# Gated delta rule inside a two-layer encoder trunk: pairs of the triangular inverse by a predicated copy, spreading copies replaced by zero-step weights, and the tail of the last head behind the first transposition

## What is computed

```python
for l in range(DEPTH):                     # DEPTH = 2
    x = x + 0.5 * swiglu(rmsnorm(x, ffn1_norm[l]), ...)        # D_FF = 2816
    x = x + hybrid_mixer(rmsnorm(x, mix_norm[l]), ...)
    x = x + 0.5 * swiglu(rmsnorm(x, ffn2_norm[l]), ...)
return rmsnorm(x, final_norm)

def hybrid_mixer(h, ...):
    proj = h @ w_in                        # q, k, v, g_out, a, b, glu, gates
    q, k, v = silu(short causal convolution of 4 taps of q, k, v), q and k l2-normed
    o = gated_delta_chunked(q, k, v, g, beta)      # 8 heads of 128
    y_a = (rmsnorm(o, head_norm) * silu(g_out)) @ w_a_out
    c = causal_depthwise_conv(val * sigmoid(gt), dw_conv_w) + dw_conv_b    # 31 taps
    y_b = silu(rmsnorm(c, conv_norm)) @ w_b_out
    return (sigmoid(gate_a) * y_a + sigmoid(gate_b) * y_b) @ w_o

def gated_delta_chunked(q, k, v, g, beta):
    gc = cumsum(g); decay = exp(gc_i - gc_j)
    m = (k * beta) @ k.T * decay_strict
    sol = triangular_solve(eye + m, [v * beta, k * beta * exp(gc)])
    attn = q @ k.T * decay_incl
    # then a scan over the chunks: v_new, o, state
```

## Time and profile before

| | us |
|---|---|
| runs of the kernel before | 3057.24, 3074.15, 3071.31 |
| median | 3071.31 |
| the profiled execution, its own time | 3066.26 |
| span of its instructions | 3064.5 |
| PE busy | 2902.3 (95%) |
| DVE busy | 1671.2 (55%) |
| ACT busy | 1107.7 (36%) |
| POOL busy | 345.8 (11%) |

### The profile page before, as it was taken

One profiled execution on the slowest core, in us unless ns is written; L12 is line 12 of the kernel. 1 busy time (PEld: TensorE's weight loads), 2 busy tenths in 40 slices (PEclk: granted clock), 3 DMA queues, 4 the chain that ended last, 5 costly groups with the idle time before them and its releaser, 6 DMA issues.

```text
span 3064.5 us, 41142 instructions
## 1 busy us (share of the span) xinstructions
PE 2902.3 (95%) x14080; PEld 2404.8 (78%) x14080; DVE 1671.2 (55%) x2475; ACT 1107.7 (36%) x1631; POOL 345.8 (11%) x308
## 2 busy tenths in 40 slices
PE   7999969999999999999999998699999999999999
PEld 6888847878887888888778886478887878788887
DVE  5554236878787345553255531388878863555532
ACT  3232235445454233322142322345554542332321
POOL 1000021211122010000000000221122220100000
PEclk9999979999999999999999999899999999999999
...
GB/s 143 96 96 96 66 106 120 104 99 103 100 108 80 101 94 91 98 97 93 78 103 96 94 95 62 115 102 99 114 105 86 117 74 106 91 94 97 94 91 69
DMA packets 479208, 296.79 MB, mean 97 GB/s; under 512 B 12180, under 2 KB 462868, under 8 KB 479092
## 3 DMA queue, kind: packets, MB, share of 16 engines
...
## 4 chain that ended last, share of the span: by engine, by line
PE 78%; issue 8%; DVE 5%; DMA 5%; ACT 3%; POOL 1%; DVEq 0%; ACTq 0%; POOLq 0%; SPq 0%
PE bank L414 76%; DMA raw<-in_w_in 4%; PE bank L542 2%; DMA w_lo<-raw 1%; ACT w_hi L751 1%; ACT w_lo L753 1%; DVE cacc L1185 1%; DVE dcol L1113 1%; DVE NT L1291 0%; DVE X L1244 0%; DVE XT L1302 0%; DVE XT L1244 0%; POOL attn L1559 0%; ACT hf L843 0%; DVE w_lo L1001 0%
## 5 line engine op out<-in xcount | busy, mean ns | idle before, releaser
L414 PE MATMUL bank<-h_hi,w_hi 128*128 128x512 f32 x2432 | 970.9, 399 | 27.8 <-DVE h_lo L1033 14.0
L414 PE MATMUL bank<-h_lo,w_hi 128*128 128x512 f32 x2432 | 984.2, 405 | 0.0
L414 PE MATMUL bank<-h_hi,w_lo 128*128 128x512 f32 x2432 | 966.0, 397 | 0.0
L751 ACT ACTIVATE w_hi<-raw 128x1024 fp32r<-128x1024 f32 x448 | 471.8, 1057 | 709.0 <-PE bank L414 621.9
L1001 DVE TENSOR_TENSOR w_lo<-raw,w_hi 128x1024 fp32r<-128x1024 f32 x336 | 412.1, 1228 | 553.9 <-ACT w_hi L751 553.0
L414 PEld LDWEIGHTS bank<-h_hi,w_hi 128*128 128x128 f32 x2432 | 463.7, 191 | 124.1 <-DVE h_lo L1033 15.5
L414 PEld LDWEIGHTS bank<-h_hi,w_lo 128*128 128x128 f32 x2432 | 463.9, 191 | 84.3
L414 PEld LDWEIGHTS bank<-h_lo,w_hi 128*128 128x128 f32 x2432 | 464.1, 191 | 82.6
L1185 DVE SCALAR_TENSOR_TENSOR cacc<-c_raw,ncol,cacc 128x512 f32<-128x512 f32 x464 | 352.4, 760 | 8.2
L414 PE MATMUL bank<-act_hi,w_hi 128*128 128x512 f32 x704 | 279.1, 396 | 0.0
L414 PE MATMUL bank<-act_lo,w_hi 128*128 128x512 f32 x704 | 279.1, 396 | 0.0
...
## 6 DMA issues: line engine op xcount, KB each, us to landing
raw<-in_w_in SPq DMA_DIRECT2D x128, 512.0 KB, 8.4
...
```

The lines of the kernel that those rows point to most:

```text
L414: return nc.tensor.matmul(o, a, b, start=start, stop=stop, **kw)
L751: nc.scalar.activation(w_hi[c % SLOTS][:, :], raw[c % SLOTS][:, :], ACT.Copy).then_inc(hi_done, 1)
```

## The change

- The gate's spread copy gbc (DVE) and the spread copies fbc (DVE, 16 in the heads and 8 in the norms) are gone. The matmuls take one column with a step of zero as their 128 columns of weights (`whole`).
- The mask decs (POOL) is gone; NT is made from the unmasked dec with a negated factor (a new small operation, neg). XT begins as the identity, which ACT writes (XTI), and one predicated copy puts the pairs in: it takes the place of m1 and x2T.
- tanh of v goes to a tile of its own, thv. Y is no longer negated.
- PE_ORDER has other places. x2t comes after 8 halves in place of 14, vt, y0 and fb behind it; four halves in place of three ahead of each xt, three in place of two ahead of os1, os2 and os3, two in place of three ahead of gr.
- On DVE the chain to x2T comes ahead of v, c_raw and dcol; the last head's oF, o_hi and o_lo move behind level 0 and 1, and the filler lists are new.
- ACT takes sgc behind kd, and X2 and level 0 ahead of the first unit's copies. POOL takes rk first.

```diff
@@ -84,29 +84,29 @@
-PE_ORDER = "H H H gr H H kt H so kk H H kq vt H H fb H H H H x2t H H H y0 H H H xy0".split()
+PE_ORDER = "H H gr H H kt kk H kq H so H H x2t vt H H y0 fb H H xy0".split()
 for _l in range(1, LEVELS):
-    PE_ORDER += f"H H H xt{_l - 1} y{_l} H H H xy{_l}".split()
+    PE_ORDER += f"H H H H xt{_l - 1} y{_l} H H H xy{_l}".split()
 PE_ORDER += "H H vn0 H H os0".split()
 for _c in range(1, NC):
-    PE_ORDER += f"H H p{_c} H H vn{_c} H H os{_c}".split()
+    PE_ORDER += f"H H p{_c} H H vn{_c} H H H os{_c}".split()
 HALVES = 12
...
-DVE_STEPS = ["hs", "gbc", "kT", "qT", "vT", "dmin", "skE", "rden", "bnk2", "NT", "m1", "x2T", "attnT"]
+DVE_STEPS = ["hs", "kT", "dmin", "qT", "skE", "rden", "bnk2", "neg", "NT", "x2T", "vT", "attnT"]
 DVE_STEPS += [f"x{_l}" for _l in range(LEVELS)]
...
     DVE_STEPS += [f"r{_c}", f"vn{_c}"] + ([f"s{_c}"] if _c < NC - 1 else [])
-DVE_TAIL = ["og", "vE", "fbc", "oF", "ohi", "olo"]
-ACT_STEPS = ["thk", "thq", "thv", "sgc", "ksq", "decT", "eg", "kd", "X2", "vs", "Y0"]
+DVE_TAIL = ["og", "vE", "oF", "ohi", "olo"]
+ACT_STEPS = ["thk", "thq", "XTI", "thv", "ksq", "decT", "eg", "kd", "sgc", "X2", "Y0", "vs"]
 for _l in range(1, LEVELS):
     ACT_STEPS += [f"XT{_l - 1}", f"Y{_l}"]
 ACT_STEPS += ["qsq"]
-POOL_STEPS = ["decs", "deci", "rk", "qd"]
+POOL_STEPS = ["rk", "deci", "qd"]
 ACT_DENSE = ["q_raw", "q_tap", "k_raw", "k_tap", "v_raw", "v_tap", "g_th", "val", "gt_th"]
...
@@ -312,9 +310,9 @@
-def spread(cols):
-    return cols.rearrange("p (c o) -> p c o", o=1).broadcast_to([P, NC, P])
+def whole(col):
+    return col.broadcast_to([P, P])
...
@@ -551,9 +549,9 @@
     if name == "gr":
-        ve("gbc")
+        ve("hs")
         for c in range(NC):
-            m = mm(bank[0][:, c * P:c * P + P], dec[:, c * P:c * P + P], incl)
+            m = mm(bank[0][:, c * P:c * P + P], whole(hs[:, HS_G, c:c + 1]), incl)
         m.then_inc(*pe_dn.step(name))
...
@@ -616,9 +614,9 @@
     else:
-        pe.wait_ge(ve_tl.sem, ve_tl.after(rn, "fbc"))
+        pe.wait_ge(po_tl.sem, po_tl.after(rn, "rs"))
         for c in range(NC):
-            m = mm(bank[5][:, c * P:c * P + P], fbc[:, c, :], ident)
+            m = mm(bank[5][:, c * P:c * P + P], whole(sm[:, 5, c:c + 1]), ident)
     m.then_inc(*pe_tl.step(name))
...
@@ -867,13 +865,19 @@
+    def level(lv):
+        if lv:
+            pe_(f"xt{lv - 1}")
+            nc.scalar.activation(XT[:, :], bank[3][:, :], ACT.Copy).then_inc(*ac_dn.step(f"XT{lv - 1}"))
+        pe_(f"y{lv}")
+        nc.scalar.activation(Y[:, :], bank[1][:, :], ACT.Copy).then_inc(*ac_dn.step(f"Y{lv}"))
     if rn is not None:
         pe_("vn3", rn - 1)
+        nc.scalar.activation(chunked(XT), each_chunk(I_ID), ACT.Copy).then_inc(*ac_dn.step("XTI"))
         act.wait_ge(ve_ds.sem, ve_ds.after(rn, "v3"))
-        nc.scalar.activation(XT[:, :], va[:, :], ACT.Tanh).then_inc(*ac_dn.step("thv"))
-        act.wait_ge(ve_tl.sem, ve_tl.after(rn - 1, "og"))
-        act.wait_ge(ve_ds.sem, ve_ds.after(rn, "sg"))
-        nc.scalar.activation(sgc[:, :], sgn[:, :], ACT.Copy).then_inc(*ac_dn.step("sgc"))
+        nc.scalar.activation(thv[:, :], va[:, :], ACT.Tanh).then_inc(*ac_dn.step("thv"))
         act.wait_ge(po_tl.sem, po_tl.after(rn - 1, "sum"))
...
@@ -885,11 +889,16 @@
         a.then_inc(*ac_dn.step("kd"))
+        act.wait_ge(ve_tl.sem, ve_tl.after(rn - 1, "og"))
+        act.wait_ge(ve_ds.sem, ve_ds.after(rn, "sg"))
+        nc.scalar.activation(sgc[:, :], sgn[:, :], ACT.Copy).then_inc(*ac_dn.step("sgc"))
+        pe_("x2t")
+        nc.scalar.activation(X[:, :], bank[0][:, :], ACT.Copy).then_inc(*ac_dn.step("X2"))
+        level(0)
     dense_steps(0, *dense)
     if rn is not None:
-        pe_("x2t")
-        nc.scalar.activation(X[:, :], bank[0][:, :], ACT.Copy).then_inc(*ac_dn.step("X2"))
         act.wait_ge(po_dn.sem, po_dn.after(rn, "rk"))
+        pe_("vt")
         for c in range(NC):
...
@@ -897,17 +906,9 @@
-    def level(lv):
-        if lv:
-            pe_(f"xt{lv - 1}")
-            nc.scalar.activation(XT[:, :], bank[3][:, :], ACT.Copy).then_inc(*ac_dn.step(f"XT{lv - 1}"))
-        pe_(f"y{lv}")
-        nc.scalar.activation(Y[:, :], bank[1][:, :], ACT.Copy, scale=-1.0).then_inc(*ac_dn.step(f"Y{lv}"))
     for t in range(1, 5):
         if rn is not None:
-            for lv in ((0, 1), (2, 3), (4, 5), ())[t - 1]:
+            for lv in ((1, 2), (3, 4), (5,), ())[t - 1]:
                 level(lv)
...
@@ -1222,15 +1217,17 @@
-    first = ("t", "t", "t", (0, 0), "t", (0, 1))
-    behind = [("t", (0, 2), "t", "t", "t", "t"), ((1, 0), "t", (1, 1), "t", (1, 2), "t"),
-              ("t", "t", "t", "t", (2, 0), "t"), ((2, 1), "t", (2, 2), "t", "t", "t"),
-              ("t", "t", "t", "t", "g", "t"), ()]
+    first = ("t", "t")
+    behind = [("t", (0, 0), "oF", (0, 1), "ohi", (0, 2)), ("olo", "t", "t", "t", "t", "t"),
+              ("t", (1, 0), "t", (1, 1), "t", (1, 2)), ("t", "t", "t", "t", "t"),
+              ((2, 0), "t", (2, 1), "t", (2, 2), "t"), ()]
     def put(items):
         for x in items:
-            if x == "t":
+            if x == "t" or x in DVE_TAIL and not (dn and before):
                 fill()
+            elif x in DVE_TAIL:
+                tail(x, rn - 1, hn - 1)
             elif x == "g":
...
@@ -1250,65 +1247,56 @@
         ts(hs[:, :, :], hsc[:, hn, :, :], 1.0, None, ALU.mult).then_inc(*ve_dn.step("hs"))
-        me("hs")
-        nc.vector.tensor_copy(chunked(dec), spread(hs[:, HS_G, :])).then_inc(*ve_dn.step("gbc"))
...
         act_of("k", ka, kT, Y)
-        if before:
-            tail("og", rn - 1)
-        act_of("q", qa, qT, X)
-        act_of("v", va, va, XT)
         pe_("gr")
...
         a.then_inc(*ve_dn.step("dmin"))
+        act_of("q", qa, qT, X)
         if before:
-            tail("vE", rn - 1)
+            tail("og", rn - 1)
         ac("ksq")
...
         tt(sm[:, 2, :], sm[:, 1, :], hs[:, HS_BETA, :], ALU.mult).then_inc(*ve_dn.step("bnk2"))
+        me("bnk2")
+        ts(sm[:, 6, :], sm[:, 2, :], -1.0, None, ALU.mult).then_inc(*ve_dn.step("neg"))
+        me("neg")
+        ac("decT")
+        pe_("kk")
+        for c in range(NC):
+            t = slice(c * P, c * P + P)
+            a = stt(out=NT[:, t], in0=bank[2][:, t], scalar=sm[:, 6, c:c + 1], in1=dec[:, t], op0=ALU.mult, op1=ALU.mult)
+        a.then_inc(*ve_dn.step("NT"))
+        me("NT")
+        ac("XTI")
+        dve.sem_inc(xy_seen, 1)
+        nc.vector.copy_predicated(chunked(XT), where(I_M1T), chunked(NT)).then_inc(*ve_dn.step("x2T"))
+        if before:
+            tail("vE", rn - 1)
+        act_of("v", va, va, thv)
         dve.wait_ge(ac_ds.sem, ac_ds.after(rn, "gt_th"))
         dve.wait_ge(taps, rn * TAPS + TAPS)
         stt(out=c_raw[:, TAPS - 1:], in0=gth[:, :], scalar=1.0, in1=valb[:, :], op0=ALU.add, op1=ALU.mult).then_inc(*ve_ds.step("craw"))
-        if before:
-            tail("fbc", rn - 1)
     if dense and dn:
         columns(*dense)
     if dn:
-        me("bnk2")
-        po_("decs")
-        pe_("kk")
-        for c in range(NC):
-            t = slice(c * P, c * P + P)
-            a = stt(out=NT[:, t], in0=bank[2][:, t], scalar=sm[:, 2, c:c + 1], in1=decs[:, t], op0=ALU.mult, op1=ALU.mult)
-        a.then_inc(*ve_dn.step("NT"))
-        if before:
-            tail("oF", rn - 1, hn - 1)
-        me("NT")
-        tt(chunked(XT), chunked(NT), each_chunk(I_M1T), ALU.mult).then_inc(*ve_dn.step("m1"))
-        if before:
-            tail("ohi", rn - 1, hn - 1)
-        else:
-            fill()
-        me("m1")
-        tt(chunked(XT), each_chunk(I_ID), chunked(XT), ALU.subtract).then_inc(*ve_dn.step("x2T"))
-        if before:
-            tail("olo", rn - 1, hn - 1)
         pe_("kq")
...
         level(lv)
-    if dn:
+    if not dn:
+        silu_gate()
+    else:
         for c in range(NC):
...
@@ -1317,7 +1305,7 @@
             ts(VN[:, :], bank[1][:, 0:P], sm[:, 2, c:c + 1], None, ALU.mult).then_inc(*ve_dn.step(f"vn{c}"))
-            fill()
+            put("g" if c == 1 else "t")
             if c < NC - 1:
...
@@ -1535,13 +1518,12 @@
             square_sum(rn - 1)
+        ve("skE")
+        tt(sm[:, 3, :], sm[:, 0, :], pw[:, 1, :], ALU.pow).then_inc(*po_dn.step("rk"))
+        if before:
             mean_root(rn - 1)
         ac("decT")
-        tt(chunked(decs), chunked(dec), each_chunk(I_STRICT), ALU.mult).then_inc(*po_dn.step("decs"))
         tt(chunked(attn), chunked(dec), each_chunk(I_INCL), ALU.mult).then_inc(*po_dn.step("deci"))
-        ve("skE")
-        tt(sm[:, 3, :], sm[:, 0, :], pw[:, 1, :], ALU.pow).then_inc(*po_dn.step("rk"))
         lo(Rd, G, c0 + 3)
```

More of the change, by code:

```diff
@@ L41 @@
 PR_DW, PR_B, PR_CN, PR_F1, PR_MIX, PR_F2, PR_QKV, PR_N = 0, 31, 32, 33, 34, 35, 36, 48
-I_ID, I_INCL, I_STRICT, I_M1T, I_LV = 0, 1, 2, 3, 4
+I_ID, I_INCL, I_M1T, I_LV = 0, 1, 2, 3
 LEVELS = 6
@@ L143, in trunk @@
         pw = sb("pw", [2, NC])
-        fbc = sb("fbc", [NC, P])
         hf = [sb(f"hf{i}", [SEQ]) for i in range(2)]
```

(22 more changed lines are left out.)

5 lines of the change are left out of this document (1 added, 4 removed).

## The result

| | kernel before | changed kernel |
|---|---|---|
| median of the runs | 3069.59 us (3057.24 to 3074.15, 4 runs) | 3101.34 us (3097.36 to 3102.94, 4 runs) |
| ratio, 95% interval | 1 | 1.0108 (1.0076 to 1.0140) |
| profiled execution: time, span | 3066.26, 3064.5 | 3099.86, 3098.0 |
| mean granted clock in the span | 0.974 | 0.967 |

The change makes the kernel slower by 31.8 us. The forecast was 22 slower, 3093, and its range held the result.

The account below looks back on a forecast made before the run. PE was taken as the bound, busy for 2902.3 of 3064.5 us. The terms, 53 + 4 + 6 - 31 - 4.6 - 5 = +22, on a median of 3071.3 gave 3093 us, range 3076 to 3112.

Parts of the forecast that it names:

- x2t, -31: At x2t in the heads: PE's 33.0 us of waits go, leaving 1 for each first head; 31 us less.
- gr, +53 and +4: At gr: taps behind the last VN delay hs, 4.4 us late twelve times (+53) and 2.0 twice (+4).
- the loop's edge, +6: At DVE's loop edge: its 17.9 us of standing now come on top of the taps; 6 us more.
- rival 1: Taps behind VN cost less: none held by POOL's sum, part of the fetch under them; +6, 3078; 15%.
- Other waits, -4.6: At xt, the last heads and the norms: 7.6 go, +2 for each layer, two spread copies saved; 4.6 less.
- Zero-step weights, 0: Weight loads with a step of zero, at gr and fb: taken to cost nothing extra, at most +29.
- The clock, 0 (-10 to +12): PE's clock in the heads: slowed stretches lost at x2t and gained at gr cancel, -10 to +12 us.
- Rival 3: Slower PE stretches after each new wait at gr, doubled at the loop's edge: +14 more, 3107; 13%.
- My sign of being wrong: In the heads: the forecast would be wrong if the granted clock moved by more than 0.02.
- The ends of waits, -5: On PE: each of 34 waits that go gives back 0.16 us more than its row says; 5 less.

Follow-up runs that it names:

- the first experiment: The changed kernel with filler places for all 31 taps ahead of the last VN: 3017.54 us, ratio 0.9844 to the kernel before.

## Why the prediction was right, and where it was not

*x2t, -31.* Right: 33.0 fell to 1.7, and the copy took 0.74 from SBUF as well, the lower of the two bounds. Of the way there, the copy was worth 11 us of wait and the rest was worth more. There was some luck in it: with PE at 2.4 GHz on its way from gr to x2t (6.95 us where I had 6.5) the waits are 5.0, as in the first experiment, and it was the slow clock behind the new waits at gr (9.3 us for the way) that hid the other 3.

*gr, +53 and +4, and the loop's edge, +6.* Together +63; the waits grew by 85.6 - 19.7 = 65.9. The eight full turns that are not at an edge waited 4.74 to 4.77 where I had 4.4, since the sum held the taps up by 1.09 and not 0.8. The Trainium skill's rule (SBUF — State Buffer, section "SBUF: two separate sides") had put it at up to 1.28, and the runs side with it. By the same rule the one that starts first keeps the ports, and the trace agrees there too: kT, which began ahead of the sum, was not held, and the sum was. The second heads (four taps) waited 2.44 for my 2.0. The four edges waited 7.25, 7.62, 9.13 and 9.37, 33.4 in all, where my terms make 34.9. There DVE stood 15.1 us for no shown reason, against 17.9 in the earlier trace rows, and 26.9 in the first experiment: this stand differs from one execution and kernel to the next, by more than my term for it. Over all profiles it is 12.0 to 18.2 in the four kernels with taps in front of it and 17.9 to 28.2 in the six without, so a part of it may well run under the taps, as rival 1 had it; no run shows that apart.

*Other waits, -4.6.* Net -3.0: the 7.6 at xt went, the norms gave 1.1, ACT's Y and the tail's fbc another 2.9, and the last heads took 4.6 (I had +4). I did not see the first heads' wait for v (2.9), nor S (1.1).

*Zero-step weights, 0.* Right as a price of the load, to the tenth of a us for fb and the norms. As a part of the change it may be worth more than I gave it: 19 us in the kernel before, most of them by way of the clock behind waits at x2t, which the change has done away with anyway.

*The clock, 0 (-10 to +12).* About 6 by the estimate from the busy time at 1.2 GHz, so within its bounds. I had let sixteen old waits and fourteen new ones cancel, and that is nearly what they did: 19 us went with the waits at x2t and some 24 came with those at gr, where 16.9 busy us at 1.2 GHz became 65.6. My premise that the longer waits slow PE more came out in this way: each of the sixteen waits at gr slowed it, for 3.4 to 10.2 us, and eleven of the sixteen at x2t, for 3.4; but a part of the longer stretches is the wait itself. Rival 3 (+14 on top, 13%) had the mechanism and twice the size. My sign of being wrong, heads whose clock moves by more than 0.02, is met by the second layer (0.97 to 0.94) and not by the first (0.97 to 0.96): it was a poor sign, since the granted clock also falls where PE stands.

*The ends of waits, -5, is the term with its reason wrong.* It counts 34 waits that go and leaves out those that come. Over the parts named here 36 went and 16 came, twenty fewer, which by its own 0.16 each is -3.

The profiled pair gives the closing sum. The waits named above changed by -31.3 + 65.9 - 3.0 = +31.6 where I had +27. PE's busy time rose by 5.2 where clock and ends had -5 together; about 6 of the clock and -3 for the ends make 3, and the other 2 are open (PE's new order is in them). That makes 36.8 for a difference of the spans of 33.5; the other 3 lie in waits of parts that the change doesn't touch. So the 9 us between +22.4 and the medians' +31.8 are no single step: 4 in the waits and 10 in PE's busy time, of which the clock is more than half, less 3 in other waits and 2 by which the profiled pair (33.5) is further apart than the medians.

The sign and most of the size came from counting places in two lists. What decided was not what the change's operations cost (the copy gained 11 us of wait, the weights cost nothing) but that its lists have 25 places for 31 taps.
